# Spreading the per-head norms of an RWKV-7 stage with TensorE matmuls in place of a round trip through DRAM

## What is computed

```
kk = heads(k * k_k)
kk = kk / jnp.maximum(jnp.sqrt(jnp.sum(kk * kk, axis=-1, keepdims=True)), 1e-12)
...
mean = jnp.mean(y, axis=-1, keepdims=True)
var = jnp.mean(jnp.square(y - mean), axis=-1, keepdims=True)
y = ((y - mean) * lax.rsqrt(var + RWKV_LN_EPS)).reshape(bsz, seq, W) * ln_w + ln_b
bonus = jnp.sum(r * k * r_k, axis=-1, keepdims=True) * v
y = (y + bonus.reshape(bsz, seq, W)) * gate
```

## Time and profile before

| what | value |
|---|---|
| median of 3 runs | 2852.69 us (2851.42 to 2854.69) |
| the profiled execution, its time | 2852.69 us |
| its span | 2851.5 us |
| PE busy | 2803.1 us, 98% of the span |
| DVE busy | 1736.9 us, 61% |
| ACT busy | 1315.4 us, 46% |
| GpSimd busy | 43.3 us, 2% |
| granted TensorE clock, mean | 0.998 |

### The profile page before, as it was taken

The page is one execution under the profiler, slowest core; times in us unless marked ns, Lnnn a source line. Parts: engine busy times, 40 slices in busy tenths (PEclk is TensorE's granted clock), DMA queues, the critical chain, the costliest instruction groups (busy, mean ns, idle before and its releaser), DMA issues.

```text
span 2851.5 us, 40994 instructions
## 1 busy us (share of the span) xinstructions
PE 2803.1 (98%) x17275; PEld 2397.4 (84%) x17275; DVE 1736.9 (61%) x2053; ACT 1315.4 (46%) x1672; POOL 43.3 (2%) x71
## 2 busy tenths in 40 slices
PE   8999899999999999999999999999999999999998
PEld 7887788788888888888888888888888888888886
DVE  6679656754445565555555566655666756665665
ACT  5444433544434443444434555645554444443444
POOL 2000000000000000000000000000000000000001
PEclk9999999999999999999999999999999999999999
DMA  7555314555545656656566555555455555555553
GB/s 233 179 174 164 104 47 150 177 178 192 178 143 182 184 188 195 187 194 190 192 192 192 188 182 186 184 163 177 157 183 194 188 194 192 183 199 194 188 182 132
DMA packets 392420, 504.60 MB, mean 177 GB/s; under 512 B 11360, under 2 KB 285293, under 8 KB 391213
## 3 DMA queue, kind: packets, MB, share of 16 engines
q1 hardware_dynamic: 385149, 490.35, 53.1%
q10 hardware_dynamic: 7088, 11.62, 1.3%
HBM read 499.77 MB, written 2.17 MB: 176 GB/s over the span
## 4 chain that ended last, share of the span: by engine, by line
PE 92%; DVE 5%; ACT 1%; DMA 1%; issue 1%; ACTq 0%; SPq 0%; DVEq 0%
PE PS L639 37%; PE PS L644 32%; PE PS L648 16%; PE PS L864 3%; DVE wlo L1883 1%; PE PS L676 1%; DVE slab L2000 1%; DMA slab<-norms 1%; PE PS L996 0%; PE PS L1012 0%; DMA slab<-in_x 0%; PE PS L1045 0%; PE PS L784 0%; ACT whi L1281 0%; PE PS L804 0%
## 5 line engine op out<-in xcount | busy, mean ns | idle before, releaser
L1883 DVE TENSOR_TENSOR wlo<-raw,whi 128x1024 fp32r<-128x1024 f32 x922 | 1127.8, 1229 | 794.8 <-ACT whi L1281 791.2
L1281 ACT ACTIVATE whi<-raw 128x1024 fp32r<-128x1024 f32 x922 | 969.9, 1057 | 954.4 <-PE PS L648 488.2
L644 PE MATMUL PS<-XX,whi 128*128 128x512 f32 (+1 forms) x3856 | 1217.9, 397 | 5.1 <-DVE wlo L1883 5.1
L648 PEld LDWEIGHTS PS<-XX,wlo 128*128 128x128 f32 (+1 forms) x3856 | 725.0, 188 | 171.5
L648 PE MATMUL PS<-XX,wlo 128*128 128x256 f32 (+1 forms) x3856 | 760.3, 278 | 0.0
L639 PE MATMUL PS<-whi,act 128*128 128x512 f32 x2240 | 602.1, 391 | 0.0
L644 PEld LDWEIGHTS PS<-XX,whi 128*128 128x128 f32 (+1 forms) x3856 | 589.9, 189 | 8.5 <-DVE wlo L1883 5.7
L639 PEld LDWEIGHTS PS<-whi,act 128*128 128x128 f32 x2240 | 418.0, 188 | 85.1
L639 PE MATMUL PS<-wlo,act 128*128 128x512 f32 x1120 | 344.9, 389 | 0.0
L639 PE MATMUL PS<-whi,XX 128*128 128x512 f32 x1024 | 279.8, 395 | 6.7 <-DVE wlo L1883 5.3
L639 PEld LDWEIGHTS PS<-wlo,act 128*128 128x128 f32 x1120 | 210.3, 188 | 44.1
(11 more groups left out here) (363 smaller groups left out, 1353.8 us busy)
## 6 DMA issues: line engine op xcount, KB each, us to landing
raw<-in_ffn_w SPq DMA_DIRECT2D x128, 1024.0 KB, 5.5
raw<-in_w_in SPq DMA_DIRECT2D x103, 1024.0 KB, 5.0
raw<-in_w_ffn_gate SPq DMA_DIRECT2D x44, 1024.0 KB, 4.9
raw<-in_w_ffn_up SPq DMA_DIRECT2D x44, 1024.0 KB, 4.8
raw<-in_w_ffn_down SPq DMA_DIRECT2D x44, 1024.0 KB, 5.1
raw<-in_w_out SPq DMA_DIRECT2D x32, 1024.0 KB, 5.1
raw<-in_xattn_wk SPq DMA_DIRECT2D x16, 1024.0 KB, 5.2
raw<-in_xattn_wv SPq DMA_DIRECT2D x16, 1024.0 KB, 4.9
```

The source lines that it names most:

```text
L644: T.matmul(ps[0:wd, f, :], whi[:, o:o + wd], b.x[:, kk, :], start=first, stop=False, skip_group_check=True)
L648: mm = T.matmul(ps[0:wd, f, 0:SEQ], wlo[:, o:o + wd], b.x[:, kk, 0:SEQ], start=False, stop=last, skip_group_check=True)
L1281: S.activation(k.whi[:, h % 4, 0:b.size], k.raw[:, t % 4, u * b.size:(u + 1) * b.size], ACT.Copy).then_inc(k.w_hi, 1)
L1883: V.tensor_tensor(k.wlo[:, h % 4, 0:b.size], k.raw[:, h // 2 % 4, u * b.size:(u + 1) * b.size], k.whi[:, h % 4, 0:b.size].bitcast(F32), AL ...
```

## The change

In both places the round trip through DRAM is replaced by `head_spread`: 8 matmuls with a stationary matrix of 16 rows (`spread`, ones where a feature belongs to a head) that repeat `hs` over the partitions in PSUM, where DVE reads it. `spread` is made once by a DVE copy from a small GpSimd constant `selT` (one memset and two selects more). In prep PE gets the spread at position 68, and "bon" waits for `kn` as well, since it writes a bank that `kn` reads. The first "tok" evacuation no longer waits for `kn`. In post the spread writes the banks that the gate writes next, so the gate waits for `fin`; the second token half runs one step behind the first; there are 10 steps; PE's waits for `sq` and `var` stand one and more steps ahead of what they were for; `ln_w` moves one step down; and the split of the result moves from position 111 to 112, behind the evacuation of the last block.

```diff
-POST_STEPS = 9
+POST_STEPS = 10
...
+def head_spread(k, src, v):
+
+    bank = 512 // v.shape[2]
+    for f in range(RP):
+        mm = k.nc.tensor.matmul(v[:, f, :], k.spread[:, f, :], src, start=f % bank == 0, stop=True,
+                                skip_group_check=True)
+    return mm
...
-    for _ in range(6):
-        yield
+    for _ in range(4):
+        yield
+    T.wait_ge(*rp.DVE("hs"))
+    head_spread(k, k.hs, k.banks(4)).then_inc(rp.pe, 1)
+    yield
+    yield
     T.wait_ge(*rp.DVE("rk"))
+    T.wait_ge(*rp.DVE("kn"))
     head_sum(k, k.t1, 4).then_inc(rp.pe, 1)
...
     mm.then_inc(ro.pe, 1)
     yield
-    yield
     T.wait_ge(*ro.DVE("sq"))
+    yield
     head_sum(k, k.pt1[:, :, tok], b0, P).then_inc(ro.pe, 1)
     yield
-    yield
-    yield
-    yield
     T.wait_ge(*ro.DVE("var"))
+    yield
+    yield
+    T.wait_ge(*ro.DVE("hs"))
+    head_spread(k, hs, v).then_inc(ro.pe, 1)
+    yield
+    T.wait_ge(*ro.DVE("fin"))
     T.wait_ge(k.g2_w, 16)
...
 def halves_of(post, k):
-    return side_by_side(*(post(k, h) for h in range(NT)))
+
+    return side_by_side(post(k, 0), a_step_behind(post(k, 1)))
+
+
+def a_step_behind(steps):
+    yield
+    yield from steps
...
-            if b.number == k.blocks_of("tok")[0].number:
-                S.wait_ge(*k.rp.DVE("kn"))
...
-    S.dma_start(k.norms_out[0], k.hs).then_inc(k.norm_stored[0], 16)
-    yield
-    norms_laid(k, 0, k.norm_rows, slice(0, SEQ))
...
-    S.dma_start(k.norms_out[1][:, P * h:P * h + P], hs).then_inc(k.norm_stored[1 + h], 16)
-    yield
-    norms_laid(k, 1 + h, k.pt1[:, :, P * h:P * h + P], slice(P * h, P * h + P))
...
 def lora_dve(k):
+    k.nc.vector.tensor_copy(k.spread.rearrange("p a (b c) -> p (a b) c", c=64),
+                            k.selT[:, :, :].rearrange("p a b -> p (a b)").unsqueeze(2).to_broadcast([16, 16, 64]))
...
-    V.wait_ge(k.norm_there[0], 32)
-    V.tensor_tensor(KK, KK, k.norm_rows, ALU.mult).then_inc(rp.dve, 1)
+    V.wait_ge(*rp.PE("nb"))
+    V.tensor_tensor(KK, KK, k.banks(4), ALU.mult).then_inc(rp.dve, 1)
...
-    V.tensor_tensor(R, R, k.bc(col["rwkv_ln_w"], P), ALU.mult).then_inc(ro.dve, 1)
-    yield
+    yield
+    k.dve(V.tensor_tensor(R, R, k.bc(col["rwkv_ln_w"], P), ALU.mult))
     V.wait_ge(*ro.ACT("sd"))
...
-    yield
-    V.wait_ge(k.norm_there[1 + h], 32)
-    V.wait_ge(*ro.DVE("lw"))
-    V.tensor_tensor(R, R, pt1, ALU.mult).then_inc(ro.dve, 1)
+    V.wait_ge(*ro.PE("rb"))
+    V.tensor_tensor(R, R, v4, ALU.mult).then_inc(ro.dve, 1)
     V.wait_ge(*ro.DVE("fin"))
-    yield
     k.dve(V.tensor_tensor(R, R, VV, ALU.add))
+    yield
     V.wait_ge(*ro.PE("gate"))
...
-    s.to(k.half_at("add", 3) - 1)
+    s.to(k.half_at("add", 3))
...
-    s.go(1)
```

More of the change, by code:

```diff
@@ L158, in __init__ @@
         self.m_ar, self.m_kr, self.m_ll = (sb(n, [P, 2, RC]) for n in ("m_ar", "m_kr", "m_ll"))
-        self.sel = sb("sel", [P, RP, 16])
+        self.sel, self.selT = sb("sel", [P, RP, 16]), sb("selT", [16, RP, 2])
         self.idc, self.rst = sb("ident_compact", [P, RC]), sb("rst", [P, SEQ])
@@ L232, in layout @@
         self.HP = slice(96, 112)
-        self.hs, self.bs = v(23568, SEQ)[self.HP, :], v(23824, SEQ)[self.HP, :]
+        self.spread, self.hs, self.bs = v(22544, RP, P)[self.HP], v(23568, SEQ)[self.HP, :], v(23824, SEQ)[self.HP, :]
         self.eend, self.DTf = v(25472, RP, NRC), v(25504, SEQ)
@@ L251, in layout @@
         self.LL, self.VA = pairs(over(3, 0, RP, P), 2), over(3, 1024, RP, P)
-        self.norm_rows = v(0, RP, SEQ)
-        self.norms_out = [self.nc.dram_tensor(f"norms{n}", (RWKV_H, SEQ), F32).ap() for n in range(2)]
         self.bonus, self.bonus_out = over(3, 0, RP, SEQ), self.nc.dram_tensor("bonus", (RWKV_H, SEQ), F32).ap()
@@ L355, in signals @@
         self.stored = sem("stored")
-        self.norm_stored, self.norm_there = ([sem(f"norm_{w}{n}") for n in range(3)] for w in ("stored", "there"))
         self.bonus_stored, self.bonus_there = sem("bonus_stored"), sem("bonus_there")
@@ L381, in signals @@
             pool="y0 y1")
-        self.rp = Stage(sem, "prep", pe="w a n2 bon",
+        self.rp = Stage(sem, "prep", pe="w a n2 nb bon",
                         dve="kr kk hs rk kn bs lwd kkd r eend end",
@@ L388, in signals @@
             dve="lr kr ll pt p1 u2 p2 p3 z0 z1 z2 z3 st", act="va x kt u2t u3 r m y") for g in range(2)]
-        self.ro = [Stage(sem, f"post{h}", pe="mb var gate", dve="cen sq var lw hs vb fin out", act="sd")
+        self.ro = [Stage(sem, f"post{h}", pe="mb var rb gate", dve="cen sq var hs vb fin out", act="sd")
                    for h in range(NT)]
@@ L954, in post_pe @@
     b0, tok = 4 + 2 * h, slice(P * h, P * h + P)
-    R, v = k.RKV[:, 0:8, tok], k.quarters(b0)
+    R, hs, v = k.RKV[:, 0:8, tok], k.hs[:, tok], k.quarters(b0)
     for g in range(2):
@@ L962, in post_pe @@
     yield
+    T.wait_ge(*ro.DVE("sq"))
     yield
-    T.wait_ge(*ro.DVE("sq"))
     head_sum(k, k.pt1[:, :, tok], b0, P).then_inc(ro.pe, 1)
     yield
+    T.wait_ge(*ro.DVE("var"))
     yield
     yield
+    T.wait_ge(*ro.DVE("hs"))
+    head_spread(k, hs, v).then_inc(ro.pe, 1)
     yield
-    T.wait_ge(*ro.DVE("var"))
+    T.wait_ge(*ro.DVE("fin"))
     T.wait_ge(k.g2_w, 16)
@@ L978, in post_pe, with halves_of @@
     yield
+def halves_of(post, k):
+    return side_by_side(post(k, 0), a_step_behind(post(k, 1)))
+def a_step_behind(steps):
     yield
-def halves_of(post, k):
-    return side_by_side(*(post(k, h) for h in range(NT)))
+    yield from steps
 def cross_pe(k, h):
@@ L1542, in lora_act @@
     yield from step_sizes_act(k)
[L1545 to L1552, removed]
 def prep_act(k):
@@ L1562, in prep_act @@
     S.activation(k.hs, k.PS[k.HP, 4, 0:SEQ], ACT.Sqrt).then_inc(rp.act, 1)
-    yield
-    yield
-    S.wait_ge(*rp.DVE("hs"))
-    S.dma_start(k.norms_out[0], k.hs).then_inc(k.norm_stored[0], 16)
-    yield
-    norms_laid(k, 0, k.norm_rows, slice(0, SEQ))
-    for _ in range(6):
+    for _ in range(9):
         yield
@@ L1629, in post_act @@
     yield
-    S.wait_ge(*ro.DVE("hs"))
-    S.dma_start(k.norms_out[1][:, P * h:P * h + P], hs).then_inc(k.norm_stored[1 + h], 16)
-    yield
-    norms_laid(k, 1 + h, k.pt1[:, :, P * h:P * h + P], slice(P * h, P * h + P))
     yield
@@ L2359, in post_dve @@
     yield
+    V.wait_ge(*ro.PE("rb"))
+    V.tensor_tensor(R, R, v4, ALU.mult).then_inc(ro.dve, 1)
+    V.wait_ge(*ro.DVE("fin"))
+    k.dve(V.tensor_tensor(R, R, VV, ALU.add))
     yield
-    V.wait_ge(k.norm_there[1 + h], 32)
-    V.wait_ge(*ro.DVE("lw"))
-    V.tensor_tensor(R, R, pt1, ALU.mult).then_inc(ro.dve, 1)
-    V.wait_ge(*ro.DVE("fin"))
-    yield
-    k.dve(V.tensor_tensor(R, R, VV, ALU.add))
     V.wait_ge(*ro.PE("gate"))
@@ L2664, in constants @@
     G.memset(k.buf1[:, :, 0:1], 0.0).then_inc(k.zeroed.pool, 1)
-    for t, v in ((k.ones, 1.0), (k.triu, 1.0), (k.negu, 0.0), (k.sel, 1.0),
+    for t, v in ((k.ones, 1.0), (k.triu, 1.0), (k.negu, 0.0), (k.sel, 1.0), (k.selT, 1.0),
                  (k.m_in, 1.0), (k.head_mean, 1.0 / 64), (k.idc, 0.0), (k.rst, 1.0), (k.m_kr, 1.0), (k.m_ll, -1.0)):
@@ L2693, in constants @@
     select(k.sel[:, :, :], [[-128, RP], [64, 16]], 63, -1, ge, 0.0)
+    select(k.selT[:, :, :], [[-2, RP], [-1, 2]], 0, 1, ge, 0.0)
+    select(k.selT[:, :, :], [[2, RP], [1, 2]], 0, -1, ge, 0.0)
     select(k.rst[:, :].rearrange("p (c e) -> p c e", e=RC), [[0, NRC], [1, RC]], -1, 0, ge, 0.0)
```

## The result

The change makes the kernel slower: 2873.09 us median (2871.9 to 2875.46, 4 runs) against 2852.06 us (2851.19 to 2854.69, 4 runs) of the kernel before in the same rounds. The ratio is 1.0074, with a 95% interval of 1.0055 to 1.0091. The forecast was 2871.4 us in a range of 2861 to 2879 us. Run a second time, beside other kernels, the change gave 2873.81 us (2872.48 to 2874.63, 4 runs), ratio 1.0068, 95% interval 1.0054 to 1.0082.

The account below looks back on a forecast made before the run. PE, busy 2803.1 of 2851.5 us, was taken to bound the kernel. From 2852.7 us, less 1.5 (prep), plus 15.4 (post's stalls and spreads less an old wait) and 4.8 (clock), came 2871.4 us, range 2861 to 2879 us.

Parts of the forecast that it names:

- The order of post's queues makes five stalls: Post, positions 97, 100, 103, 104 and 112: new PE waits of 2.0, 3.7, 2.2, 3.7 and 1.9 us, 13.5 us together.
- The spreads are paid by their columns: Prep and post: 16-row matmuls cost by columns, not rows, 3.6 us in each, 7.2 us together as upper value.
- Prep gives 1.5 us: Prep: spread hides in PE's idle time; gain 0.7 us with a slow stretch, 1.7 us without, 1.5 us taken.
- the 0.9 us of wait for half 71: Prep: PE, after half 70 ends at 232.2 us, waits 0.9 us for half 71's `wlo`, until 233.1 us.
- The replay: Engine queues stepped through from profile rows; in prep it has the spread ending at 223.6 us.
- The trips cost PE 1.7 us in each place: Prep and post: the norms' DRAM trips cost the end some 1.7 us in each, not the chain's 18.6 us.
- The clock in post: Post: three new stalls each bring a slow stretch of lowered clock, 3 x 1.6 = 4.8 us, bounds 0 and 8.
- the middling waits: Post: the three shorter stalls of 2.0, 2.2 and 1.9 us, of which one was counted as bringing a slow stretch.
- No change: Rival: PE's waits in post are met, only new work and old stalls count, 2853.1 us; chance 0.07.
- Faster: Rival: 16-row matmuls cost next to nothing and waits in post and prep come back, 2844.3 us; chance 0.04.
- At most one slow stretch: Rival: post's stalls as forecast, but at most one slow stretch, 2866.6 to 2868.2 us; chance 0.22.

Follow-up runs that it names:

- experiment 2: The changed kernel with post's steps placed by the replay (9 steps, both token halves together, split at 111), all spreads kept: 2859.71 us, ratio 1.0023.
- experiment 3: The changed kernel with PE's waits for `sq` and `var` moved to where they are needed: 2868.81 us, ratio 1.0054.
- experiment 4: The changed kernel with `fin` reading an SBUF tile, so the gates need not wait for it; post's norms left out: 2866.13 us, ratio 1.0044.
- experiment 5: The changed kernel with the split of the result put back at position 111: 2870.78 us, ratio 1.0057.
- experiment 1: The kernel before with only the prep part of the change, post as it was: 2852.58 us, ratio 0.9998.
- experiment 9: The kernel before with only the prep part, its spread over 128 rows and the norms kept: 2851.7 us, ratio 0.9992.
- experiment 7: The kernel before with only the prep part, its spread over 128 rows, prep's norms left out: 2851.86 us, ratio 0.9993.
- experiment 8: The changed kernel with post's steps placed by the replay, all spreads over 128 rows, norms left out: 2855.58 us, ratio 1.0005.
- experiment 10: The changed kernel with post's steps placed by the replay, spreads over 128 rows, norms kept: 2855.21 us, ratio 1.0007.

## Why the prediction was right, point by point

- **The order of post's queues makes five stalls.** Forecast 2.0, 3.7, 2.2, 3.7 and 1.9 us, 13.5 us together; measured 1.78, 3.76, 1.97, 3.58 and 1.79 us, 12.9 us, each with the releaser that was named. Shown by experiments 2 (other places: 13.4 us less with the same work), 3, 4 and 5.
- **The spreads are paid by their columns.** Forecast 3.6 us in prep and 3.6 in post; measured 3.72 us, and 2.05 us twice in the rows of post (1.98 us from its start at 488.09 us to the start of the half behind it). Where the clock falls within it, as in experiment 1, the one in prep takes up to 4.95 us. Over 128 rows it is 3.62 us: rows outside the 16 cost no time. (The prediction puts the sum 7.2 us lower if a spread were free; its own sum holds only the 3.6 us of post, and the 3.6 us of prep stand in the cover of waits.) By the Trainium skill ("TensorE: Matmul & The Clock Gate", section "LDWEIGHTS (loading the stationary operand)") the row count does not matter for a load; the traces agree as to the duration of the whole group at full clock, 3.72 and 3.62 us.
- **Prep gives 1.5 us.** It gave 1.9 us up to the scan in the first profiled execution of the change. Of all seven traces with the 16-row spread in prep two gave 1.8 or 1.9 us and five 1.1 us; the forecast had 0.7 us with a slow stretch and 1.7 us without. The mechanism is right only in part. The waits of 2.06 and 2.09 us vanished as forecast, but the 0.9 us of wait for half 71 did not appear, because PE came there late: it had its slow stretch earlier, behind the spread. In experiment 9, where the clock stays up, that wait is there, 1.08 us at 232.98 us (forecast until 233.1 us), and "bon" starts at 236.40 us (forecast 236.6 us). The replay was right for a clock that did not fall, and prep gives 1.9 us there.
- **The trips cost PE 1.7 us in each place.** Shown for neither. In prep 1.73 us is DVE's wait for the norms. In post the timeline of DVE before has no wait for a DMA at all, and PE's 1.71 us is a wait for `wlo`, which stood behind the normalising of `mem` in DVE's queue:

```profile
502.39 3.26 DVE L2029 TENSOR_SCALAR slab<-slab,stat 128x512 f32<-128x512 f32 x8
```

The sum does not hang on this, since it takes the 1.71 us off for the reason that PE comes later, and the wait did go.
- **The clock in post.** Forecast three slow stretches at 1.6 us, 4.8 us; there were two, behind the waits of 3.76 and 3.58 us. The price of one was right in the first profiled execution, 5.47 - 3.73 = 1.7 us in the second gate, and too low in the second, 6.50 - 3.73 = 2.8 us. Behind 1.78, 1.97 and 1.79 us the clock stayed at 1.00, so none of the middling waits counted. This term was mis-sized: one stretch fewer, and 0.04 x 80.4 = 3.2 us in place of 4.8 us in the first execution. In the second execution the two stretches alone cost some 5.5 us.
- **What the sum left out.** Post took 20.1 us more, forecast 15.4 + 4.8 = 20.2. By rows it is 12.9 us of stalls less 1.7 us, 4.0 us of spreads and 3.2 us of clock, 18.4 us. Most of the other 1.7 us lie in the 16 halves of the stretch, at the places where a group or a wait now cuts in: from start to start the halves take 47.3 us in all, of which 1.5 us are the clock's, where they took 44.4 us. (A pair of matmuls ahead of a wait counts 0.61 us where it is 0.46 us to the next start, and the first four behind one take 1.00 us to the next start in place of 0.90 us.) That the total fits better than its terms is luck: in the second execution post took 22.1 us more.
- **The 1.7 us by which the median is over the forecast** have no place of their own. In the first profiled execution the scan took 2.7 us longer and post 20.1 us; in the second it was 1.1 and 22.1 us. The scan's code is the same. All the kernels have a wait of 2.36 to 2.37 us in it, and the clock of the window from 350 to 360 us goes, if not exactly, with the length of the scan: 0.83 in the kernel before with a scan of 142.16 us, 0.83 in the second execution of the change with 143.26 us, 0.72 in the first with 144.87 us. The largest and the smallest of the other kernels are experiment 9 with 144.77 us and experiment 7 with 141.32 us:

```profile
350.00:360.00 10.00, 7.63 (x94) 7.38 (x91) 3.61 (x9) 1.01 (x2) 0.00 (x0) 0.67 0.01 2
```

```profile
350.00:360.00 10.00, 7.63 (x180) 7.43 (x176) 5.81 (x13) 1.01 (x2) 0.00 (x0) 1.00 0.01 2
```

- **No rival came true.** "No change" fell with the stalls at `var` and `fin`, which stand behind an evacuation that needs PE's own last half. "Faster" fell with the spreads' 2.0 us each. "At most one slow stretch" has one fewer than there were.

## What to carry to other kernels

On in-order queues, ask of a new wait what stands in the other engine's queue ahead of the awaited instruction, and whether one of these needs work of the waiting engine itself: if so it is a stall whatever the speed; the five here were counted beforehand to 0.3 us each. A round trip through DRAM that is long in the chain may cost the bounding engine little (taking the one out of prep gave at most 1.9 us), while its replacement adds work to that very engine. New PE work can also cost more than its own duration, by the clock behind it: read both in a trace of that work in its place.

## What the hardware did that I had not expected

- **Matmuls over 16 rows (partitions 96 to 111) bring the clock down, with PE busy throughout.** In all seven traces with the 16-row spread in prep the window from 220 to 230 us reads 0.66 to 0.83, and in its slow part the clock is at its lower level of 1.2 GHz (0.50); in all four traces with 128 rows it reads 1.00, at the same place and length. The pair of 16-row spreads in post, 4 us in all, did it too (0.66 from 480 to 490 us); the single ones of 2 us in the change, 10.7 us from start to start, did not. The Trainium skill ("TensorE: Matmul & The Clock Gate", section "What's actually happening") has the level set by how busy PE was; here PE had no idle time in the 10 us, so busy as the profile counts it does not keep the clock up. Filling the other rows keeps it, for one DVE memset of 0.27 us and two GpSimd memsets among the constants: 4.1 us less in experiment 8 and 4.5 us less in experiment 10 than in experiment 2. Few columns do not have this effect: the head sum of the kernel before, with a stationary operand of 128 rows and 16 columns, takes 3.61 us, and the matmuls behind it run at full clock (0.62 to 0.63 us for a pair). Why the rows have this effect no run here shows.

```profile
192.86 3.61 PE L804 MATMUL PS<-slab,sel 128*16 128x256 f32 x16 [0.55 <-ACT slab L1558]
196.41 0.73 PE L644 MATMUL PS<-XX,whi 128*128 128x512 f32 x2
...
197.21 0.63 PE L644 MATMUL PS<-XX,whi 128*128 128x512 f32 x2
```

- **The same wait does not always have the same effect.** Behind the wait of 2.36 to 2.37 us in the scan the clock stayed at 1.00 in two of the twelve traces and fell in ten (0.67 to 0.83 from 350 to 360 us). The scan took 141.3 to 141.6 us in the two and 142.2 to 144.9 us in the ten, with PE busy some 126.5 us in the two and 128.1 or 129.7 us in the others. The two are experiments 7 and 8, which move other numbers through the scan, so one trace each can't tell the data from chance; but the runs of experiment 9, with the norms kept, cover the same range of times (2850.0 to 2853.62 us) as those of experiment 7 (2849.84 to 2853.6 us). Behind 1.7 to 2.0 us in post the clock never fell, behind 3.58 us and more always, and the slow stretch there cost some 1.5 to 2.8 us. The two profiled executions of the change differ by 0.8 us in prep, 1.6 us in the scan and 2.0 us in post, partly against each other, and that is the reason why 2 us can't be shown from a few runs.
